# The prologue of a two-block transformer kernel, normalised and transposed one token tile at a time

## The reference

```python
def rms_norm(x, g, eps=NORM_EPS):
    xf = x.astype(jnp.float32)
    y = xf * lax.rsqrt(jnp.mean(xf * xf, axis=-1, keepdims=True) + eps)
    return (y * g.astype(jnp.float32)).astype(x.dtype)

h = rms_norm(x, norm1_g[l])          # x: 1 x 256 x 1024
proj = h @ w_in[l]                   # 1024 x 9,000-odd columns, split among four branches
```

## Time and profile before

| | |
|---|---|
| median of 3 executions | 1259.69 us (1259.63 to 1259.81) |
| profiled execution, time | 1258.78 us |
| profiled execution, span | 1257.0 us |
| PE busy | 1242.1 us, 99% |
| POOL busy | 941.9 us, 75% |
| ACT busy | 650.2 us, 52% |
| DVE busy | 490.8 us, 39% |

### The profile page before, as it was taken

How to read it: one execution, slowest core, us unless ns; L and a number is a source line. 1 busy time by engine, 2 the same in 40 slices (tenths; PEclk the granted TensorE clock), 3 DMA queues, 4 the chain that set the end, 5 groups by cost and what they waited for, 6 DMA issues and landing times.

```text
span 1257.0 us, 18537 instructions
## 1 busy us (share of the span) xinstructions
PE 1242.1 (99%) x7547; PEld 1073.6 (85%) x7547; DVE 490.8 (39%) x893; ACT 650.2 (52%) x873; POOL 941.9 (75%) x409
## 2 busy tenths in 40 slices
PE   9999999999999999999999999999999989999998
PEld 7988888888888888899899888888879868888886
DVE  5535334552224320037662153332042674333125
ACT  5583555755457653444544464444345655444433
POOL 6956357746969889875589698888967667888974
PEclk9999999999999999999999999999999999999999
DMA  8735235534646666653455676665638434565651
GB/s 285 215 119 168 69 101 167 183 106 142 221 144 208 188 198 203 199 166 114 151 168 198 200 232 187 197 186 189 209 129 271 161 118 154 188 187 192 201 167 67
DMA packets 147738, 218.33 MB, mean 174 GB/s; under 512 B 9367, under 2 KB 79558, under 8 KB 147654
## 3 DMA queue, kind: packets, MB, share of 16 engines
q1 hardware_dynamic: 143664, 209.73, 52.5%
q10 hardware_dynamic: 3990, 7.42, 1.8%
HBM read 216.07 MB, written 1.05 MB: 173 GB/s over the span
## 4 chain that ended last, share of the span: by engine, by line
PE 94%; DVE 4%; ACT 1%; issue 1%; POOL 0%; POOLq 0%; DVEq 0%; ACTq 0%
PE acc L1954 18%; PE acc L1982 12%; PE acc L1984 12%; PE acc L1983 12%; PE acc L1958 9%; PE pm L1998 6%; PE acc L1989 4%; PE acc L1992 4%; PE acc L1991 4%; PE acc L1922 2%; PE acc L1923 1%; PE acc L1924 1%; PE acc L2185 1%; PE acc L2011 1%; PE acc L2187 1%; PE acc L2186 1%
## 5 line engine op out<-in xcount | busy, mean ns | idle before, releaser
L582 POOL TENSOR_TENSOR wlo<-raw,whi 128x1024 fp32r<-128x1024 f32 (+4 forms) x404 | 941.2, 2356 | 303.0 <-ACT whi L596 300.6
L596 ACT ACTIVATE whi<-raw 128x1024 fp32r<-128x1024 f32 (+4 forms) x404 | 404.3, 1033 | 217.1 <-PE acc L1984 139.8
L1954 PE MATMUL acc<-XT,whi 128*128 128x512 f32 x960 | 240.6, 392 | 0.0
L1954 PEld LDWEIGHTS acc<-XT,whi 128*128 128x128 f32 x960 | 172.7, 189 | 31.0
L1958 PEld LDWEIGHTS acc<-XT,wlo 128*128 128x128 f32 x960 | 131.0, 190 | 9.4
L1958 PE MATMUL acc<-XT,wlo 128*128 128x256 f32 x960 | 133.9, 282 | 0.0
L1989 PE MATMUL acc<-XT,whi 128*128 128x256 f32 x432 | 123.2, 285 | 0.0
L1982 PE MATMUL acc<-whi,XT 128*128 128x512 f32 (+4 forms) x320 | 123.1, 385 | 0.1
L1991 PE MATMUL acc<-XT,whi 128*128 128x256 f32 x432 | 122.2, 283 | 0.0
L1992 PE MATMUL acc<-XT,wlo 128*128 128x256 f32 x432 | 122.2, 283 | 0.0
L1984 PE MATMUL acc<-whi,XT 128*128 128x512 f32 (+4 forms) x320 | 119.4, 373 | 0.0
(11 more groups left out here) (413 smaller groups left out, 1961.0 us busy)
## 6 DMA issues: line engine op xcount, KB each, us to landing
raw<-in_w_in SPq DMA_DIRECT2D x68, 512.0 KB, 3.5
raw<-in_w_ff SPq DMA_DIRECT2D x64, 512.0 KB, 3.8
raw<-in_w_gate SPq DMA_DIRECT2D x44, 512.0 KB, 3.6
raw<-in_w_up SPq DMA_DIRECT2D x44, 512.0 KB, 3.5
raw<-in_w_down SPq DMA_DIRECT2D x44, 512.0 KB, 3.9
raw<-in_w_in_mix SPq DMA_DIRECT2D x36, 512.0 KB, 3.4
raw<-in_w_branch SPq DMA_DIRECT2D x16, 512.0 KB, 3.7
raw<-in_w_out_mix SPq DMA_DIRECT2D x16, 512.0 KB, 3.2
```

What stands on the lines that cost most here:

```text
L582: nc.gpsimd.tensor_tensor(piece(wlo, u), piece(raw, u), piece(whi, u).bitcast(F32), ALU.subtract).then_inc(S["w_lo"], 1)
L596: return nc.scalar.activation(out_, in_, func, **k)
L1954: T.matmul(acc[:, n % 2, f, :], piece(whi, u)[:, i, f * P:(f + 1) * P], XT[:, :, k0 + i, :], start=k0 + i == 0, stop=False)
```

## The change

The input is handled by token tile. Each tile gets its own sum of squares, root and refinement; VectorE multiplies the tile itself by its root into `XN1` (tile 0 in one instruction, tile 1 in two halves), and TensorE transposes `XN1` with the identity, eight blocks a tile, where it made 16 products with a diagonal matrix. The `scale` matrices and the `eye` transpose go. The tables of rows are turned in a bank of `acc` and no longer in `pm`. On ScalarE's queue the head of the constants is issued first, then the two tables; positions, `heads` and `o_g` move to SP's queue, around the rest of the constants, between weight units 3 and 4. ScalarE copies the columns between the root of tile 0 and the sum of squares of tile 1. The waiting matmuls are 18, 8 and 4 where they were 28 and 8.

```diff
@@ sync
                 if u == 4:
+                    sp_.dma_start(posi[:], a["positions"]).then_inc(S["p0_in"], 16)
                     sp_.dma_start(ct[:, HEAD_COLS:], a["consts"][:, HEAD_COLS:]).then_inc(S["k_in"], 16)
+                    sp_.dma_start(heads[:], a["heads"].partition_broadcast(P)).then_inc(S["c_in"], 16)
+                    sp_.dma_start(o_g[:], a["dn_out_norm_g"].partition_broadcast(P)).then_inc(S["c_in"], 16)
@@ scalar
+            act.dma_start(ct[:, 0:HEAD_COLS], a["consts"][:, 0:HEAD_COLS]).then_inc(S["id_in"], 16)
             act.dma_start(rowsA[0:n_a, :], a["rows_a"]).then_inc(S["r_in"], 16)
             act.dma_start(rowsB[0:n_b, :], a["rows_b"]).then_inc(S["r_in"], 16)
-            act.dma_start(ct[:, 0:HEAD_COLS], a["consts"][:, 0:HEAD_COLS]).then_inc(S["id_in"], 16)
-            act.dma_start(posi[:], a["positions"]).then_inc(S["p0_in"], 16)
-            act.dma_start(heads[:], a["heads"].partition_broadcast(P)).then_inc(S["c_in"], 16)
-            act.dma_start(o_g[:], a["dn_out_norm_g"].partition_broadcast(P)).then_inc(S["c_in"], 16)
             logs()
             act.wait_ge(S["x_in"], 16)
-            fn(XN1[:, 0, :], X[:, 0, :], ACT.Square, accum_out=ss[:, 0:1])
+            link(fn(XN1[:, 0, :], X[:, 0, :], ACT.Square, accum_out=ss[:, 0:1]))
+            act.wait_ge(S["id_in"], 16)
+            rstd(rs[:, 0:1], ss[:, 0:1], D, eps6).then_inc(S["rstd"], 1)
+            act.wait_ge(S["cols"], 1)
+            fn(colA[:], acc[:, 0, 0, 0:n_a], ACT.Copy)
+            fn(colB[:], acc[:, 0, 0, P:P + n_b], ACT.Copy).then_inc(S["cols"], 1)
             act.wait_ge(S["x1_in"], 16)
             link(fn(XN1[:, 1, :], X[:, 1, :], ACT.Square, accum_out=ss[:, 1:2]))
-            act.wait_ge(S["id_in"], 16)
-            rstd(rs[:, 0:NT], ss[:, 0:NT], D, eps6).then_inc(S["rstd"], 1)
-
-            act.wait_ge(S["cols"], 1)
-            fn(colA[:], pm[:, 0, 0:n_a], ACT.Copy)
-            fn(colB[:], pm[:, 0, P:P + n_b], ACT.Copy).then_inc(S["cols"], 1)
+            rstd(rs[:, 1:2], ss[:, 1:2], D, eps6).then_inc(S["rstd"], 1)
@@ vector
-            v.wait_ge(S["rstd"], 1)
-            link(variance(rv[:, 0:NT], ss[:, 0:NT], D, 1e-6))
-            refine_columns(0, NT)
-            v.wait_ge(S["eye"], 1)
             for t in range(NT):
-                last = V.tensor_scalar(scale[:, t, :], pm[:, 3, 0:P], rs[:, t:t + 1], None, ALU.mult)
-            last.then_inc(S["xn"], 1)
+                v.wait_ge(S["rstd"], t + 1)
+                link(variance(rv[:, t:t + 1], ss[:, t:t + 1], D, 1e-6))
+                refine_columns(t, 1)
+                for h in range(t + 1):
+                    cols = slice(h * W, (h + 1) * W) if t else slice(0, D)
+                    V.tensor_scalar(XN1[:, t, cols], X[:, t, cols], rs[:, t:t + 1], None, ALU.mult)\
+                        .then_inc(S["xn"], 1)
@@ tensor
-            keep_busy(28)
+            keep_busy(18)
             pe.wait_ge(S["id_in"], 16)
-            T.transpose(pm[:, 3, 0:P], ident, ident).then_inc(S["eye"], 1)
             pe.wait_ge(S["r_in"], 32)
-            T.transpose(pm[:, 0, 0:n_a], rowsA[0:n_a, :], ident[0:n_a, 0:n_a])
-            T.transpose(pm[:, 0, P:P + n_b], rowsB[0:n_b, :], ident[0:n_b, 0:n_b]).then_inc(S["cols"], 1)
+            T.transpose(acc[:, 0, 0, 0:n_a], rowsA[0:n_a, :], ident[0:n_a, 0:n_a])
+            T.transpose(acc[:, 0, 0, P:P + n_b], rowsB[0:n_b, :], ident[0:n_b, 0:n_b]).then_inc(S["cols"], 1)
             keep_busy(8)
-            pe.wait_ge(S["x1_in"], 16)
+            for t in range(NT):
+                for k in range(KD):
+                    if k % 4 == 0 and (t or k == 0):
+                        pe.wait_ge(S["xn"], t + k // 4 + 1)
+                    last = T.transpose(pm[:, k // 2, (k % 2) * TOK + t * P:(k % 2) * TOK + (t + 1) * P],
+                                       XN1[:, t, k * P:(k + 1) * P], ident)
+                    if t and k % 2:
+                        last.then_inc(S["t_pe"], 1)
+                if t == 0:
+                    keep_busy(4)
             pe.wait_ge(S["cols"], 2)
-            pe.wait_ge(S["xn"], 1)
-            for k in range(KD):
-                for t in range(NT):
-                    last = T.matmul(pm[:, k // 2, (k % 2) * TOK + t * P:(k % 2) * TOK + (t + 1) * P],
-                                    X[:, t, k * P:(k + 1) * P], scale[:, t, :], start=True, stop=True)
-                if k % 2:
-                    last.then_inc(S["t_pe"], 1)
             product("dq", XThi, XTlo, ready=turned("x1"))
```

More of the change, by code:

```diff
@@ L419, in build @@
         sw = dn[:, 10, 0:W].rearrange("p (g s) -> p g s", g=4)
-        scale = dn[:, 9, 0:NT * P].rearrange("p (t s) -> p t s", t=NT)
         d_sq = dn[:, 7:9, :].rearrange("p a b -> p (a b)")
@@ L434, in build @@
         pm = ctx.enter_context(nc.psum_tensor("pm", [P, 4, BANK], F32))
-        names = """p0_in f_rows x_in x1_in id_in r_in eye c_in k_in w_hi w_lo w_used evac0 evac1 t_pe t_hi t_lo rstd xn cols dn_sq
+        names = """p0_in f_rows x_in x1_in id_in r_in c_in k_in w_hi w_lo w_used evac0 evac1 t_pe t_hi t_lo rstd xn cols dn_sq
             still dn_l2 dn_rn dn_qkn sp_in sp_e dn_g dn_gc dn_gcs dn_gex dn_rows dn_e0 dn_egr dn_e dn_kk dn_lt dn_kv
@@ L679, in _ @@
             high_halves(AHEAD)
-            act.wait_ge(S["xn"], 1)
+            act.wait_ge(S["xn"], 3)
             act.dma_start(sw[:], a["sg_w_s"].rearrange("g t s -> t g s")).then_inc(S["s_w"], 16)
```

## The result

The changed kernel takes 1264.28 us (median of 7 executions, 1262.13 to 1265.98) against 1259.69 before (7 executions, 1259.22 to 1260.10): a ratio of 1.0039, 95% interval 1.003 to 1.0048. The forecast was 1261.1, its range ended at 1264.2, and the chance for slower by over 0.2% was 0.28. The profiled execution took 1265.79, 7.0 more than that of before (1258.78), with a span of 1264.0.

The account below looks back on a forecast made before the run. TensorE was taken to bound the kernel from the first `dq` matmul; its start moving from 15.61 to 17.0 gave +1.4 us, so 1259.69 + 1.4 = 1261.1 us, range 1258.9 to 1264.2.

Parts of the forecast that it names:

- TensorE bounds, and a shift at the first product goes through: From the first `dq` matmul on, TensorE is the bound; a shift of that start moves the end by as much.
- the landing of the tables: On ScalarE's queue, the tables, now last of three transfers, were taken to land at 9.2 us.
- its 17.0: The forecast start in us of the first `dq` matmul on TensorE, against 15.61 before.
- the late tables: Rival: each us of landing after 9.2 is a us on the product; with 12, +4.2, 1263.9; chance 0.11.
- The wait for the columns ahead of tile 1's square: ScalarE waits for the columns while tile 1, there at 7.87, lies idle; its square starts at 10.2.
- From the tables' landing to the first product: The prologue's steps from the tables at 9.2 through square, root, scaled copy and first low halves to `dq` at 17.0.
- The blocked copy: GpSimd's instruction holds the second half of VectorE's scaled copy of tile 1: 2.62 us from 13.41, until 16.03.
- The clock: Rival: TensorE's granted clock falls in its late prologue idle times, +3.1 us, 1262.8; chance 0.17.
- The moved small transfers at nothing: Positions, `heads` and `o_g`, moved to SP's queue, were put at 0, bound 0 to 0.3.

Follow-up runs that it names:

- Experiment 2: Also called before_ct_first: the kernel before with only the head of the constants issued ahead of the two tables on ScalarE's queue; 1264.20 us, ratio 1.003.
- experiment 3: The changed kernel with only the 73-row table padded with zeros to 80 rows; 1258.92 us, a single execution.
- padded: The changed kernel with both tables padded with zeros, to 80 and 112 rows; 1259.25 us, ratio to before 1.0001.
- padded_square_first: The changed kernel with both tables padded and ScalarE's wait for the columns put behind tile 1's square and root; 1258.12 us, ratio to before 0.9983.
- busy_38: The changed kernel with 38 waiting matmuls ahead of the tables instead of 18; 1265.21 us, ratio to before 1.004.
- tables_first: The changed kernel with the two tables issued ahead of the head of the constants on ScalarE's queue; 1261.78 us, ratio to before 1.0014.
- experiment 5: Also called one_copy: the changed kernel with tile 1's scaled copy in one instruction instead of two; 1265.56 us, ratio to before 1.0044.
- Before_padded: The kernel before with both tables padded to 80 and 112 rows and nothing else; 1259.00 us, ratio to before 0.9996.
- padded_square_first_less: As padded_square_first, with 2 and 1 waiting matmuls instead of 8 and 4; 1256.64 us, ratio to before 0.9972.

## Why the prediction was wrong

- **TensorE bounds, and a shift at the first product goes through.** Right: 5.7 us at the start, 5.85 at 1041. In each of the eleven traces the shift against the kernel before is at 600 what it is at 60, within 0.05 us.
- **The step that failed: the landing of the tables.** "The third of the three landed at 9.2 before, with the same bytes ahead of it as the tables have now, so I take 9.2 for the tables." It was 12.39, which is 3.2 of the 4.3 us by which the first product missed its 17.0. Bytes in the queue are the wrong measure. The constants are 128 rows and spread over 16 rings; of the tables, one is 73 rows in a single ring. Experiment 2 shows that exchanging them is enough (tables at about 12.5), experiment 3 that seven rows of padding are enough to take 4.3 us back, and the shares show that it is one ring's worth of the tables: five of the seven were in by 8.03, near the 7.47 of the padded tables in the same order. Why that ring is 4.2 us later (12.39 for 8.24) when the 73 rows go out 0.44 us later and behind the constants is argued, not shown: it then has more to share with the input and the weights, which by then are flowing. The trace agrees with the rule of the Trainium skill that I set beside the late tables (DMA: Bandwidth & Descriptors, section "Why a DMA increments its semaphore by 16 and not by 1"): no number from 2 to 16 divides 73, and it is one share; 16 divides 80, and it is sixteen. I had written that no row of mine showed it and gave the case 0.11. It was the case, a landing above 12, for which I had worked out 1263.9.
- **The wait for the columns ahead of tile 1's square.** Right in kind: ScalarE waited 6.67 us with the tile landed at about 7.3. With the tables early the wait still cost, at most the 0.7 us by which the first product moved between padded and padded_square_first.
- **From the tables' landing to the first product.** Forecast 7.8 us (9.2 to 17.0). In busy_38, on a full clock, it was 7.4 (the landing at 13.0, the product at 20.35), in tables_first 7.7 from the constants' landing. In the changed kernel 8.9 (12.39 to 21.26), by the half clock: the other 1.1 of the 4.3 us.
- **The blocked copy.** Right: the second half took 2.58 us where the forecast had 2.62. But in the changed kernel it was not the last link, as the forecast had it; TensorE on the half clock was. And GpSimd's start lay 0.05 us behind VectorE's and not 0.18, on which experiment 5 foundered.
- **The clock.** I had it as a rival, from idle times of 1.9 and 0.4 us late in the prologue; in their place stood an idle of 5.67 us ahead of the tables, where I had 1.4 (7.9 to 9.3). The late tables made 3.2 of the difference, and the 18 waiting matmuls, which ended at 6.86 and not at 7.9, the rest. The half clock cost 1.5 us in the prologue. Late tables and a fallen clock were priced as alternatives; they come together, since the one makes the idle time of the other.
- **The moved small transfers at nothing.** Right: experiment 2, without that move, has the tables as late, and in the changed kernel the positions are there for the cast at 24.1.
- **The rest.** At 1042 the half clock lasted 6.8 us instead of 3.4. Before_padded and padded_square_first show 6.8 there, too, without late tables, padded 3.4, and one_copy none: it does not follow the change. The longer half clock explains the difference between 5.85 and 7.0 in the profiled execution. Why the median of seven lies 4.6 over, not 5.7, is open; only one of the seven is profiled. In the kernels without late tables the medians follow the first product within 0.6 us (padded_square_first_less: 3.1 and 3.2). The range's upper end of 1264.2 is 0.4 above the sum of its own terms (1262.8 and 1 us); it was still below the measured 1264.28.

## What to carry to other kernels

Ask of each early transfer how many rows it has, not how many bytes: a 36 KB table of 73 rows in a queue held one share of what came behind it for microseconds, and a transfer is there only with its last share. Padding both tables to a multiple of 16 brought the changed kernel 5.0 us; tile by tile, compared on equal terms, brought 1.4. In the kernel before the padding alone brought nothing clear of noise, as TensorE's waiting matmuls were the limit: it pays only with what waits for it. In a queue that runs in order, put the wait for the later input behind all work that does not need it. A float32 SBUF-to-SBUF scaling on VectorE that has not started when GpSimd begins waits out a whole GpSimd instruction, as in six of these kernels; let it be over before.

## What the runs showed of the hardware

The same three transfers in another order moved the last landing from 9.2 to 12.5 us (before against before_ct_first). Padding both tables brought the second input tile in by 6.1 instead of 7.9 us as well (ScalarE squares it without a wait at 6.36 in before_padded, and at 7.87 before), and the constants in before_padded at about 7.7 instead of 9.2. A table of 73 rows landed as one share, 102 rows as six, 80 or 112 as sixteen, and of a transfer the slowest share decided. In an idle time of 5.67 us TensorE's granted clock fell to 0.50 and stayed there for 6.8 us, 5.5 of them after the work had begun again. An idle 2.11 us went with 0.51 for 3.4 us in tables_first; an idle 2.00 us left it at 1.00 in before_ct_first.
